# A hybrid decoder step on one core: the input projection's convolution runs one tile behind the eviction, and the delta block's last transfers are issued in the next block

## The chip, the cores and the metric

The kernel runs on one core of a Trainium2 chip. It is one program for one inference step; the metric is the device time of one execution in microseconds (us), lower is better. Five engines work on it, each through its own queue and in its order: TensorE (PE) for matmuls, with its weight loads (PEld) recorded apart; VectorE (DVE) and ScalarE (ACT) for elementwise work; GpSimd (POOL); SyncE (SP), which only issues transfers here. They wait for each other by semaphores.

## The reference, cut to what matters

The step computes two decoder layers for 512 prompt tokens and 8 sample tokens (520 columns in all) with a model width of 1024. The change touches the first layer's token mixer, a gated DeltaNet:

```python
proj = hn @ w_in                                   # hn = rms_norm(h); w_in is (1024, 4112)
qkv, z, a, b = jnp.split(proj, [A_QKV, A_QKV + A_HEADS * A_DV, A_QKV + A_HEADS * A_DV + A_HEADS], axis=-1)
full = jnp.concatenate([conv_buf, qkv], axis=1)    # 3 earlier rows ahead of it
out = sum(full[:, j:j + T] * w[j] for j in range(4))   # causal convolution, 4 taps
q, k, v = jnp.split(jax.nn.silu(out), ...)         # 8 heads of 128 each
g = -jnp.exp(A_log) * jax.nn.softplus(a + dt_bias); beta = jax.nn.sigmoid(b)
o, S = gated_delta(q, k, v, g, beta, S0)           # chunked for the prompt, one step for the samples
o = rms_norm(o, o_norm) * jax.nn.silu(z)
h = h + o @ w_out
```

The new delta states of prompt and samples and the last three rows ahead of the convolution are outputs too. After it come a dense SwiGLU, the shared keys and values, windowed attention, and an expert SwiGLU.

## The kernel before, in words

All activations lie transposed: features on the 128 partitions, 520 token columns along the free axis. Float32 products are made from three products of rounded parts: each weight and each activation is split into a high part (`w_hi`, `x_hi`, a rounding copy on ScalarE) and a low part (`w_lo`, `x_lo`, raw minus high, on VectorE), and `three_products` (L225) issues high x high, high x low, low x high, each as two matmuls of 260 columns. With 8 k-tiles an output tile of 128 features takes 48 matmuls.

Weights are streamed in chunks of 2048 elements a partition (`Stream`, L234; two output tiles for all 8 k-tiles, 1 MB, two transfers of 512 KB). There are two buffers each for raw, high and low. `load_chunk` (L202) waits on `lo_done`, so a raw buffer is filled again when the low half of the chunk two before is made. `split_hi` (L261, its instruction L265) and `split_lo` (L267, L270) make the parts.

The program is a row of blocks; a block ends on all engines before the next begins. Those around the change:

- `load_phase` (L382): inputs are loaded and turned, the first chunk is split. It clears `ab_raw`, the padded weights of the gates a and b (128 columns wide, 16 of them used), and issues their load.
- `project_in_phase` (L504): 16 chunks, 32 output tiles: 24 for q, k, v, 8 for z. PE runs `square_tensor` (L290), with the gates' product (`narrow_product`, L649) ahead of tile 1, and the wait for its eviction ahead of tile 3. The PSUM slot of a tile is t % 4. VectorE evicts a tile times the rms factor into `u` (L596), and convolves it: last tap (L615), three taps (L617), a copy of 11 edge columns (L619), the 8 sample columns' state term (L620). ScalarE puts the SiLU of `y` into `qkv` (L546) or, for z, of `u` into `z` (L577). `u` and `y` have two buffers. The order in a turn of the loop, for two chunks j: ScalarE waits for PE to be done with chunk j - 1, splits the high half of chunk j + 1, and then runs the SiLU of the chunk's two tiles; VectorE makes the low half of chunk j + 1 and then evicts and convolves the two tiles. The first four tiles are written out; the rest is a hardware loop, to tile 23 on ScalarE and VectorE and to tile 31 on PE. POOL issues two 512 KB stores of zeros after each of the first 20 convolved tiles (`expert_out`, L522). Behind tile 23 follow the gates' small steps (L563 to L570 on ScalarE, L627 to L643 on VectorE).
- `delta_phase` (L754): the delta rule for prompt and samples. SyncE's last steps are the stores of the sample states (L855), the load of the second chunk of `a_w_out` (`sp_next`), and the two stores of the prompt state (L860).
- `add_to_residual_phase` (L1652): four chunks, eight tiles of `a_w_out`. It begins with the split of chunk 0 (2048 elements at once) and of the eight tiles of its input (`Split`, L1629; instructions L1638 on ScalarE, L1649 on VectorE). SyncE loads the other chunks and, in `before_dense`, the dense stage's first.
- `dense_phase` (L1728) and what follows is not touched.

## Time and profile before

| | us |
|---|---|
| median of 3 runs | 1709.34 |
| lowest and highest | 1706.22 to 1710.46 |
| the profiled execution | 1708.81 |
| its span, first to last instruction | 1707.0 |
| PE busy in it | 1524.8 (89%) |
| VectorE, ScalarE busy | 951.7 (56%), 630.1 (37%) |
| mean granted TensorE clock | 0.926 of full speed |

The profile comes from one profiled execution. Its time is 1.8 us above its span, the part ahead of the first and behind the last recorded instruction. The busy shares are means over stages with different limits, and a PE that is shown busy may run at half its clock, so the stages have to be read one by one.

### The profile page before, as it was taken

To read this page: it belongs to the slowest core of one execution; us is meant where nothing else is said; L and a number is where in the kernel's file an instruction comes from. 1 tells how busy PE (TensorE), PEld (TensorE's weight loads), DVE (VectorE), ACT (ScalarE), POOL (GpSimd) and SP (SyncE) were. 2 spreads that over 40 slices of the span, in tenths; PEclk is the share of its full clock that TensorE was granted. 3 is DMA by queue.
4 is the path that set the end of the run, shared out by engine and by line. 5 is a ranking of instruction groups with operands and counts; after the bars stand their busy time and mean duration, and the time that the engine had idled before them with its cause. 6 is when DMAs were issued, how large, how long until landed. Compare 5 with 4: busy or idle time off the path is not lost. (4 is left out here: it accounts for less than half of the span.)

```text
span 1707.0 us, 32531 instructions
## 1 busy us (share of the span) xinstructions
PE 1524.8 (89%) x13432; PEld 1357.4 (80%) x13432; DVE 951.7 (56%) x1285; ACT 630.1 (37%) x1055; POOL 177.5 (10%) x199
## 2 busy tenths in 40 slices
PE   6988798899979999999999986467978999999994
PEld 6988797898879999999999954356876777777773
DVE  5666635666455444444345235591345677777766
ACT  4222234442143222222333110471343556566561
POOL 0111004653102000000110000000000100000002
PEclk8999998999889999999999976696878999999997
DMA  6466213000342333332333200200424888888886
GB/s 189 182 227 225 105 43 94 2 2 3 100 136 75 99 98 88 84 91 75 95 115 102 97 1 22 84 1 1 130 84 145 274 298 284 288 286 279 274 295 230
DMA packets 165509, 226.36 MB, mean 133 GB/s; under 512 B 11145, under 2 KB 130466, under 8 KB 165194
## 3 DMA queue, kind: packets, MB, share of 16 engines
q1 hardware_dynamic: 156022, 191.81, 35.1%
q0 software_dynamic: 8512, 30.48, 4.8%
q10 hardware_dynamic: 862, 2.50, 0.4%
q8 instruction: 80, 1.31, 0.3%
q14 instruction: 33, 0.26, 0.0%
HBM read 189.15 MB, written 37.88 MB: 133 GB/s over the span
## 5 line engine op out<-in xcount | busy, mean ns | idle before, releaser
L270 DVE TENSOR_TENSOR w_lo<-w_raw,w_hi 128x2048 fp32r<-128x2048 f32 x68 | 155.9, 2293 | 127.6 <-ACT w_hi L265 127.5
L265 ACT ACTIVATE w_hi<-w_raw 128x2048 fp32r<-128x2048 f32 x68 | 129.6, 1906 | 143.0 <-PE P L229 134.3
L229 PE MATMUL P<-xf_hi,w_hi 128*128 128x260 f32 x704 | 141.8, 282 | 2.0 <-DVEq L1815 1.2
L229 PE MATMUL P<-xf_hi,w_lo 128*128 128x260 f32 x704 | 141.9, 283 | 0.0
L229 PE MATMUL P<-xf_lo,w_hi 128*128 128x260 f32 x704 | 141.7, 283 | 0.0
L229 PE MATMUL P<-xa_hi,w_hi 128*128 128x260 f32 x512 | 107.9, 293 | 23.2 <-DVE w_lo L270 20.4
L229 PEld LDWEIGHTS P<-xf_hi,w_hi 128*128 128x128 f32 x704 | 108.5, 188 | 2.6 <-issue 1.4
L229 PEld LDWEIGHTS P<-xf_hi,w_lo 128*128 128x128 f32 x704 | 108.6, 188 | 0.0
L229 PEld LDWEIGHTS P<-xf_lo,w_hi 128*128 128x128 f32 x704 | 108.2, 188 | 0.0
L229 PE MATMUL P<-xa_hi,w_lo 128*128 128x260 f32 x512 | 106.3, 290 | 0.0
L229 PE MATMUL P<-xa_lo,w_hi 128*128 128x260 f32 x512 | 105.9, 289 | 0.0
L229 PEld LDWEIGHTS P<-xa_hi,w_hi 128*128 128x128 f32 x512 | 82.6, 197 | 25.3 <-issue 25.3
L2146 PE MATMUL P<-w_hi,xb_hi 128*128 128x512 f32 x344 | 102.6, 401 | 0.0
L1899 DVE TENSOR_TENSOR w_lo<-raw_more_moe,w_hi 128x1024 fp32r<-128x1024 f32 x64 | 77.1, 1223 | 41.9 <-ACT w_hi L1893 41.3
L1899 DVE TENSOR_TENSOR w_lo<-w_raw,w_hi 128x1024 fp32r<-128x1024 f32 x64 | 77.0, 1223 | 25.7 <-ACT w_hi L1893 24.8
L1893 ACT ACTIVATE w_hi<-raw_more_moe 128x1024 fp32r<-128x1024 f32 x64 | 66.1, 1054 | 45.7 <-DMA raw_more_moe<-in_moe_w_gu_dram 18.7
L229 PEld LDWEIGHTS P<-xa_lo,w_hi 128*128 128x128 f32 x512 | 82.1, 196 | 0.0
L229 PEld LDWEIGHTS P<-xa_hi,w_lo 128*128 128x128 f32 x512 | 82.0, 196 | 0.0
L1893 ACT ACTIVATE w_hi<-w_raw 128x1024 fp32r<-128x1024 f32 x64 | 67.1, 1059 | 33.2 <-DMA w_raw<-in_moe_w_gu_dram 17.0
L2025 POOL DMA_INDIRECT xb_lo<-token_rows,index x16 | 18.9, 1179 | 568.0 <-DVE index L2423 403.1
L2146 PEld LDWEIGHTS P<-w_hi,xb_hi 128*128 128x128 f32 x344 | 62.0, 188 | 19.1 <-issue 6.2
L229 PE MATMUL P<-f_hi,w_hi 128*128 128x260 f32 x352 | 70.9, 283 | 0.0
(546 smaller groups left out, 3426.8 us busy)
## 6 DMA issues: line engine op xcount, KB each, us to landing
raw_more_moe<-in_moe_w_gu_dram SPq DMA_DIRECT2D x64, 512.0 KB, 5.2
w_raw<-in_moe_w_gu_dram SPq DMA_DIRECT2D x64, 512.0 KB, 5.4
w_raw<-in_dense_w_gu_dram SPq DMA_DIRECT2D x44, 512.0 KB, 4.7
expert_out<-zeros POOLq DMA_DIRECT2D x40, 512.0 KB, 3.8
w_raw<-in_a_w_in_dram SPq DMA_DIRECT2D x32, 512.0 KB, 5.0
raw_more_moe<-in_moe_w_down_dram SPq DMA_DIRECT2D x32, 512.0 KB, 5.6
w_raw<-in_moe_w_down_dram SPq DMA_DIRECT2D x32, 512.0 KB, 5.0
w_raw<-in_dense_w_down_dram SPq DMA_DIRECT2D x16, 384.0 KB, 4.1
```

The costliest lines, as they stand in the source:

```text
L229: ins = nc.tensor.matmul(out[:, b], w, x[:, b * HALF:(b + 1) * HALF], start=(first and n == 0), stop=(last and n == 2))
L265: nc.scalar.activation(c.w_hi[:, j % 2], c.w_raw[:, j % 2], ACT.Copy).then_inc(c.hi_done, 1)
L270: nc.vector.tensor_tensor(c.w_lo[:, j % 2], c.w_raw[:, j % 2], c.w_hi[:, j % 2].bitcast(F32), ALU.subtract).then_inc(c.lo_done, 1)
L1893: nc.scalar.activation(self.hi[m % 6], self.raw[s], ACT.Copy).then_inc(self.hi_done, 1)
L1899: nc.vector.tensor_tensor(self.lo[m % 6], self.raw[m % len(self.raw)], self.hi[m % 6].bitcast(F32), ALU.subtract).then_inc(self.lo_done, 1)
L2025: pool.indirect_dma_start(out=to, out_offset=None, in_=xs[:, :], in_offset=bass.IndirectOffsetOnAxis(ap=at, axis=0)).then_inc(x_loaded[e % ...
L2146: ins = pe.matmul(c.P[:, bank + b], a[:, t], x[:, b * 512:(b + 1) * 512], start=(t == 0 and x is w_hi and a is hi), stop=(t == KT - 1 and ...
```

## The change

In the input projection:

- PE's loop is written out for all 32 tiles; the gates' product goes from ahead of tile 1 to ahead of tile 2. `square_tensor` is gone.
- ScalarE, after each eviction, copies the edge and starts `y` with the last tap (a copy scaled by a factor per partition; both were VectorE's). At odd tiles it then makes the high half of the chunk two behind the tile's own, and then, as at even tiles, the SiLU of the tile before.
- VectorE evicts tile t, then convolves tile t - 1 (state columns, three taps), and at odd tiles makes the low half. The five state operations go behind the first two splits. The gates' first steps go to tile 1, the others behind tile 27.
- `u` and `y` have three buffers instead of two; the gates' padded weights are 64 columns wide instead of 128.

At the end of the delta block SyncE's last four issues (two weight transfers of chunk 1, two stores of the prompt state) move into the next block, ahead of `st.rest`. In that block the first chunk and its low half are split in two halves of 1024 elements, and PE waits for the second one at k-tile 4.

```diff
         def _(pe):
-            def gates():
-                pe.wait_ge(ab_lo_ready, 1)
-                narrow_product(nc, pe, slot(c, 3), L.ab_hi, L.ab_lo, c).then_inc(ab_ready, 1)
-
-            def gates_taken():
-                pe.wait_ge(ab_taken, 1)
-            square_tensor(nc, c, pe, st, ready, evacuated, inward, {1: gates, 3: gates_taken})
+            for t in range(2 * st.n):
+                l = t // 2
+                if t % 2 == 0:
+                    pe.wait_ge(c.lo_done, st.number(0, l) + 1)
+                if t == 2:
+                    pe.wait_ge(ab_lo_ready, 1)
+                    narrow_product(nc, pe, slot(c, 3)[0:64], L.ab_hi, L.ab_lo, c).then_inc(ab_ready, 1)
+                if t == 3:
+                    pe.wait_ge(ab_taken, 1)
+                pe.wait_ge(evacuated, t + 1)
+                for k in range(KT):
+                    if t == 0:
+                        inward.wait_tile(c, pe, k)
+                    at = k * 256 + t % 2 * 128
...
-            def silu(m, y):
-                nc.scalar.activation(L.qkv[:, m], L.y[:, y], ACT.Silu).then_inc(y_free, 1)
-
...
-                for j in range(2):
-                    if not first or j:
-                        act.wait_ge(ready, i * 4 + 2 * j)
-                    st.split_hi(nc, c, act, i, j + 1)
-                    if first and j == 0:
-                        act.wait_ge(L.ab_loaded, 32)
-                        nc.scalar.activation(L.ab_hi[:], L.ab_raw[:], ACT.Copy).then_inc(ab_hi_ready, 1)
-                    for m in range(2):
-                        g = 2 * j + m
-                        act.wait_ge(convolved, i * 4 + (g + 1))
-                        silu(i * 4 + g, g % 2)
-            from_first(act, NQKV // 4, qkv)
-
-            act.wait_ge(ab_taken, 1)
+            def split(l):
+                if l < st.n:
+                    if l > 1:
+                        act.wait_ge(ready, 2 * l - 2)
+                    st.split_hi(nc, c, act, 0, l)
+
+            def start_convolution(t):
+                act.wait_ge(evacuated, t + 5)
+                if t >= 3:
+                    act.wait_ge(silu_done, t - 2)
+                u = L.u[:, t % 3]
+                nc.scalar.activation(L.edge[:, t], u[:, TP:TP + 11], ACT.Copy)
+                nc.scalar.activation(L.y[:, t % 3], u[:, 3:3 + NT], ACT.Copy,
+                                     scale=L.conv_w[:, 3 * NQKV + t:3 * NQKV + t + 1]).then_inc(y_started, 1)
+
+            def silu(t):
+                act.wait_ge(convolved, t + 1)
+                nc.scalar.activation(L.qkv[:, t], L.y[:, t % 3], ACT.Silu).then_inc(silu_done, 1)
+
+            split(1)
+            act.wait_ge(L.ab_loaded, 32)
+            nc.scalar.activation(L.ab_hi[:], L.ab_raw[:], ACT.Copy).then_inc(ab_hi_ready, 1)
+            for t in range(NQKV):
+                start_convolution(t)
+                if t % 2:
+                    split((t + 3) // 2)
+                if t:
+                    silu(t - 1)
             nc.scalar.activation(gb[32:40, :], ab[32:40], ACT.Sigmoid).then_inc(act_step, 1)
             nc.scalar.activation(L.a_rate[:], L.a_log[:], ACT.Exp).then_inc(act_step, 1)
-            act.wait_ge(ready, NQKV)
-            st.split_hi(nc, c, act, 0, NQKV // 2 + 1)
             act.wait_ge(dve_step, 3)
             nc.scalar.activation(t2, t2, ACT.Exp).then_inc(own_a, 1)
             act.wait_ge(own_a, 1)
             nc.scalar.activation(t2, t2, ACT.Ln, bias=1.0).then_inc(act_step, 1)
-            for l in range(NQKV // 2, st.n):
-                if NQKV // 2 < l < last:
-                    act.wait_ge(ready, 2 * l)
-                    st.split_hi(nc, c, act, 0, l + 1)
-                for t in (2 * l, 2 * l + 1):
-                    act.wait_ge(evacuated, t + 5)
-                    nc.scalar.activation(L.z[:, t - NQKV], L.u[:, t % 2, 3:3 + NT], ACT.Silu).then_inc(z_done, 1)
+            silu(NQKV - 1)
+            for t in range(NQKV, 2 * st.n):
+                act.wait_ge(evacuated, t + 5)
+                if t % 2:
+                    split((t + 3) // 2)
+                nc.scalar.activation(L.z[:, t - NQKV], L.u[:, t % 3, 3:3 + NT], ACT.Silu).then_inc(z_done, 1)
 
         @block.vector
         def _(dve):
@@ -583,6 +573,33 @@
             for k in range(KT):
...
+            def take(t):
+                dve.wait_ge(ready, t + 1)
+                if t >= 3:
+                    dve.wait_ge(convolved, min(t - 2, NQKV))
+                if t >= NQKV + 3:
+                    dve.wait_ge(z_done, t - NQKV - 2)
+                nc.vector.tensor_tensor(halves(L.u[:, t % 3, 3:3 + NT]), slot(c, t % 4), halves(rstd), ALU.mult).then_inc(evacuated, 1)
+
+            def convolve(t):
+                u, y = L.u[:, t % 3], L.y[:, t % 3]
+                dve.wait_ge(evacuated, t + 5)
+                dve.wait_ge(y_started, t + 1)
+                nc.vector.tensor_tensor(y[:, TP:NT], y[:, TP:NT], L.from_state[:, t], ALU.add)
+                for tap in (2, 1, 0):
+                    ins = nc.vector.scalar_tensor_tensor(y[:, 0:TP], u[:, tap:tap + TP],
+                                                         L.conv_w[:, tap * NQKV + t:tap * NQKV + t + 1], y[:, 0:TP], ALU.mult, ALU.add)
+                    if tap:
+                        chain.link(ins)
+                ins.then_inc(convolved, 1)
+
+            split(1)
+            dve.wait_ge(ab_hi_ready, 1)
+            nc.vector.tensor_tensor(L.ab_lo[:], L.ab_raw[:], L.ab_hi[:].bitcast(F32), ALU.subtract).then_inc(ab_lo_ready, 1)
             sw = lambda j: L.conv_w[:, j * NQKV:(j + 1) * NQKV].unsqueeze(2).broadcast_to([128, NQKV, TS])
             rows = L.conv_state[:].rearrange("p m (b j) -> p m b j", j=3)
             chain = Chain(dve, own)
...
-            def take(t, g):
-                nc.vector.tensor_tensor(halves(L.u[:, g % 2, 3:3 + NT]), slot(c, g), halves(rstd), ALU.mult).then_inc(evacuated, 1)
-
...
-                    if first and j == 0:
-                        dve.wait_ge(ab_hi_ready, 1)
-                        nc.vector.tensor_tensor(L.ab_lo[:], L.ab_raw[:], L.ab_hi[:].bitcast(F32), ALU.subtract)\
-                            .then_inc(ab_lo_ready, 1)
-                    for m in range(2):
-                        g = 2 * j + m
-                        u, y = L.u[:, g % 2], L.y[:, g % 2]
-                        tile = lambda t: t[:, ds(i * 4 + g, 1)].rearrange("p a t -> p (a t)")
-                        w = lambda tap: L.conv_w[:, ds(i * 4 + (tap * NQKV + g), 1)]
-                        dve.wait_ge(ready, i * 4 + (g + 1))
-                        take(i * 4 + g, g)
-                        dve.wait_ge(evacuated, i * 4 + (g + 5))
-                        dve.wait_ge(y_free, i * 4 + (g + 1))
-                        chain.link(nc.vector.tensor_scalar(y, u[:, 3:3 + NT], w(3), None, ALU.mult))
-                        for tap in (2, 1, 0):
-                            chain.link(nc.vector.scalar_tensor_tensor(
-                                y[:, 0:TP], u[:, tap:tap + TP], w(tap), y[:, 0:TP], ALU.mult, ALU.add))
-                        chain.link(nc.vector.tensor_copy(tile(L.edge), u[:, TP:TP + 11]))
-                        nc.vector.tensor_tensor(y[:, TP:NT], y[:, TP:NT], tile(L.from_state), ALU.add).then_inc(convolved, 1)
-                        if first and g == 0:
-                            dve.wait_ge(ab_ready, 1)
-                            nc.vector.tensor_tensor(halves(ab), slot(c, 3)[0:40], halves(rstd[0:40]), ALU.mult).then_inc(ab_taken, 1)
-            from_first(dve, NQKV // 4, qkv)
...
+            for t in range(NQKV + 1):
+                take(t)
+                if t:
+                    convolve(t - 1)
+                if t % 2:
+                    split((t + 3) // 2)
+                if t == 1:
+                    dve.wait_ge(ab_ready, 1)
+                    nc.vector.tensor_tensor(halves(ab), slot(c, 3)[0:40], halves(rstd[0:40]), ALU.mult).then_inc(ab_taken, 1)
+                    dve.wait_ge(ab_taken, 1)
+                    step.link(nc.vector.tensor_scalar(t1, t1, L.dt_bias[:], None, ALU.add))
+                    step.link(nc.vector.tensor_scalar(t2, t1, -1.0, None, ALU.mult))
+                    step.link(nc.vector.tensor_tensor(t2, t2, t1, ALU.min))
+            for t in range(NQKV + 1, 2 * st.n):
+                take(t)
+                if t % 2:
+                    split((t + 3) // 2)
+                if t == NQKV + 3:
...
@@ -847,17 +837,13 @@
             sp.wait_ge(edge_stored, 48)
             sp.wait_ge(s_scaled, 6)
             sp.wait_ge(s_masked, 2)
-            sp_next(sp, 0)
+            sp_next(sp)
             for q in (1, 3, 5, 7):
                 k, gp, _ = outers[q]
                 sp.wait_ge(s_updated, 2 * (q + 1))
                 for h in (4 * k + 2 * gp, 4 * k + 2 * gp + 1):
                     sp.dma_start(io["new_delta_sample"][0, :, h].rearrange("b k v -> k b v"), S[:, h * TS:(h + 1) * TS])\
                         .then_inc(s_stored, 16)
-            sp_next(sp, 1)
-            for g in both:
-                chain[g].after(sp, NCH - 1, dve="S")
-                sp.dma_start(io["new_delta_prompt"][0, 0, heads(g)].rearrange("h k v -> k h v"), big("S", g, NCH)).then_inc(stored, 16)
 
         @block.gpsimd
         def _(pool):
...
         def _(pe):
-            square_tensor(nc, c, pe, st, ready, evacuated, split)
+            for t in range(2 * st.n):
+                l = t // 2
+                if t % 2 == 0 and l:
+                    pe.wait_ge(c.lo_done, st.number(0, l) + 1)
+                pe.wait_ge(evacuated, t + 1)
+                for k in range(KT):
+                    if t == 0:
+                        if k == 0:
+                            pe.wait_ge(lo_half, 1)
+                        if k == KT // 2:
+                            pe.wait_ge(c.lo_done, st.number(0, 0) + 1)
+                        split.wait_tile(c, pe, k)
+                    at = k * 256 + t % 2 * 128
+                    ins = three_products(nc, slot(c, t % 4), c.w_hi[:, l % 2, at:at + 128], c.w_lo[:, l % 2, at:at + 128],
+                                         c.x_hi[:, k], c.x_lo[:, k], k == 0, k == KT - 1)
+                ins.then_inc(ready, 1)
 
         @block.scalar
         def _(act):
-            st.split_hi(nc, c, act, 0, 0)
-            split.scalar(nc, c, act)
+            act.wait_ge(c.raw_loaded[0], 32 * (st.base // 2 + 1))
+            nc.scalar.activation(c.w_hi[parts[0]], c.w_raw[parts[0]], ACT.Copy).then_inc(hi_half, 1)
+            split.high(nc, c, act, range(0, 1))
+            nc.scalar.activation(c.w_hi[parts[1]], c.w_raw[parts[1]], ACT.Copy).then_inc(c.hi_done, 1)
+            split.high(nc, c, act, range(1, KT))
             for l in range(st.n):
                 if l:
                     act.wait_ge(ready, 2 * l)
@@ -1682,8 +1685,12 @@
         @block.vector
         def _(dve):
             dve.sem_inc(evacuated, 4)
-            st.split_lo(nc, c, dve, 0, 0)
-            split.vector(nc, c, dve)
+            dve.wait_ge(hi_half, 1)
+            nc.vector.tensor_tensor(c.w_lo[parts[0]], c.w_raw[parts[0]], c.w_hi[parts[0]].bitcast(F32), ALU.subtract).then_inc(lo_half, 1)
+            split.low(nc, c, dve, range(0, 2))
+            dve.wait_ge(c.hi_done, st.base + 1)
+            nc.vector.tensor_tensor(c.w_lo[parts[1]], c.w_raw[parts[1]], c.w_hi[parts[1]].bitcast(F32), ALU.subtract).then_inc(c.lo_done, 1)
+            split.low(nc, c, dve, range(2, KT))
             for l in range(st.n):
                 if l + 1 < st.n:
...
-            ab_at = gate_at - 3 * KT * 128 * 4
-            L.ab_raw, L.ab_hi, L.ab_lo = (placed(nc, name, [128, KT, 128], dt, ab_at + i * KT * 128 * 4)
+            ab_at = gate_at - 3 * KT * 64 * 4
+            L.ab_raw, L.ab_hi, L.ab_lo = (placed(nc, name, [128, KT, 64], dt, ab_at + i * KT * 64 * 4)
...
-                    L.u, L.y, L.from_state = alloc(inner, u=[128, 2, 3 + NT], y=[128, 2, NT], from_state=[128, NQKV, TS])
+                    L.u, L.y, L.from_state = alloc(inner, u=[128, 3, 3 + NT], y=[128, 3, NT], from_state=[128, NQKV, TS])
                     project_in_phase(nc, c, Handover(c, "in", VA, (c.x_hi, c.x_lo), None, range(KT)), s_in, L, ys)
...
-                delta_phase(nc, c, io, L, lambda sp, j: s_out.load_first(c, sp, j))
+                delta_phase(nc, c, io, L, lambda sp: s_out.load_first(c, sp, 0))
             old = nc.allocated_since(before)
...
+            def at_first(sp):
+                s_out.load_first(c, sp, 1)
+                for g in range(2):
+                    sp.dma_start(io["new_delta_prompt"][0, 0, HL * g:HL * g + HL].rearrange("h k v -> k h v"),
+                                 L.delta[g]["S"][NCH % 2]).then_inc(L.stored, 16)
+
             def before_dense(sp):
                 s_gu.start(c, sp)
                 sp.wait_ge(L.s_stored, 16 * AH)
                 sp.wait_ge(L.stored, 32)
-            add_to_residual_phase(nc, c, "a_out", s_out, before_dense, Split(c, L.qkv[:, 2 * AH:3 * AH]), to_dense, s_gu)
+            add_to_residual_phase(nc, c, "a_out", s_out, at_first, before_dense, Split(c, L.qkv[:, 2 * AH:3 * AH]), to_dense, s_gu)
         [c.late] = alloc(whole, constants_late=[128, NCST - NEARLY])
         L.router, L.r_bias = alloc(whole, router=[128, KT, NE], r_bias=[128, NE])
```

## Rows read from the trace of the kernel before

**Rows 1.** Of the page: chain by engine, granted clock by slices, issues with us to landing.
```profile
PE 27%; DVE 1%; DMA 1%; issue 0%; ACT 0%; POOL 0%; SPq 0%; ACTq 0%; DVEq 0%; POOLq 0%
...
PEclk8999998999889999999999976696878999999997
...
w_raw<-in_a_w_in_dram SPq DMA_DIRECT2D x32, 512.0 KB, 5.0
```

**Rows 2.** Windows: stretch, PE, PEld, DVE, ACT, POOL busy (instructions), clock, DMA share, GB/s.
```profile
23.40:249.52 226.12, 202.96 (x1584) 200.54 (x1584) 139.62 (x212) 59.65 (x62) 21.77 (x40) 0.95 0.43 158
...
46.60:68.30 21.70, 21.70 (x183) 21.70 (x183) 15.92 (x24) 5.52 (x5) 3.17 (x6) 1.00 0.52 194
...
82.17:96.21 14.04, 11.77 (x96) 11.57 (x96) 9.72 (x17) 3.08 (x3) 2.16 (x4) 1.00 0.61 224
...
237.98:249.52 11.54, 11.50 (x96) 11.29 (x94) 1.40 (x3) 1.28 (x2) 0.00 (x0) 1.00 0.00 0
...
482.50:487.20 4.70, 4.66 (x21) 4.69 (x22) 4.70 (x8) 2.97 (x4) 0.00 (x0) 0.50 0.72 223
...
600.00:650.00 50.00, 50.00 (x418) 50.00 (x418) 20.25 (x21) 12.35 (x12) 0.00 (x0) 1.00 0.37 104
...
1400.00:1450.00 50.00, 50.00 (x395) 35.60 (x395) 37.17 (x35) 31.51 (x32) 1.82 (x2) 1.00 0.88 293
```

**Rows 3.** Waits of PE in the projection: us in total, times, longest.
```profile
PE P L229 <- DVE w_lo L270: 20.4, 10, 5.7
```

**Rows 4.** Timeline of one turn, VectorE and ScalarE: start, us, engine, line.
```profile
82.17 0.69 DVE L596 TENSOR_TENSOR u<-P,scratch 128x520 f32<-128x520 f32 x1
...
83.00 0.49 DVE L615 TENSOR_SCALAR y<-u,conv_w 128x520 f32<-128x520 f32 x1
...
83.64 2.54 DVE L617 SCALAR_TENSOR_TENSOR y<-u,conv_w,y 128x512 f32<-128x512 f32 x3
...
91.52 0.64 ACT L546 ACTIVATE qkv<-y 128x520 f32 x1 [3.95 <-DVE y L620]
...
92.07 1.90 ACT L265 ACTIVATE w_hi<-w_raw 128x2048 fp32r<-128x2048 f32 x1
...
94.00 2.29 DVE L270 TENSOR_TENSOR w_lo<-w_raw,w_hi 128x2048 fp32r<-128x2048 f32 x1 [2.60 <-ACT w_hi L265]
96.21 0.69 DVE L596 TENSOR_TENSOR u<-P,scratch 128x520 f32<-128x520 f32 x1
```

**Rows 5.** Timeline of the projection's start and its last eviction.
```profile
28.51 1.05 ACT L555 ACTIVATE ab_hi<-ab_raw 128x1024 fp32r<-128x1024 f32 x1
...
30.36 0.40 PE L229 MATMUL P<-xa_hi,w_lo 128*128 128x260 f32 x2
...
32.21 1.22 DVE L604 TENSOR_TENSOR ab_lo<-ab_raw,ab_hi 128x1024 fp32r<-128x1024 f32 x1
...
249.52 0.70 DVE L596 TENSOR_TENSOR u<-P,scratch 128x520 f32<-128x520 f32 x1 [5.07 <-PE P L229]
```

**Rows 6.** Timeline of ScalarE's gate steps.
```profile
204.51 1.28 ACT L563 ACT_TABLE_LOAD   x1
...
207.75 0.20 ACT L564 ACTIVATE a_rate<-a_log 8x1 f32<-8x1 f32 x1
```

**Rows 7.** Timeline of the delta block's end and the next block's start.
```profile
472.96 2.73 SPq L216 DMA_DIRECT2D w_raw<-in_a_w_out_dram  x2
...
474.70 0.75 DVE L1492 SCALAR_TENSOR_TENSOR qkv<-P,vec,z 128x512 f32<-128x512 f32 x1 [0.50 <-PE P L974]
475.73 1.40 SPq L860 DMA_DIRECT2D out_dram<-delta_front  x2
477.55 1.91 ACT L265 ACTIVATE w_hi<-w_raw 128x2048 fp32r<-128x2048 f32 x1 [6.62 <-PEq L837]
...
481.70 4.96 DVE L1649 TENSOR_TENSOR xo_lo<-qkv,xo_hi 128x520 fp32r<-128x520 f32 x8
...
482.54 0.77 PE L229 MATMUL P<-xo_hi,w_hi 128*128 128x260 f32 x2 [7.88 <-DVE xo_lo L1649]
...
499.42 0.71 ACT L331 ACTIVATE xf_hi<-h,vec 128x520 fp32r<-128x520 f32 x1
```

More of the change, by code:

```diff
@@ L287, in from_first @@
             body(i, False)
-def square_tensor(nc, c, pe, st, ready, evacuated, norm=None, before={}):
-    def body(i, first):
-        for j in range(2):
-            pe.wait_ge(c.lo_done, st.number(i, j) + 1)
-            for m in range(2):
-                g = 2 * j + m
-                if first and g in before:
-                    before[g]()
-                pe.wait_ge(evacuated, i * 4 + (g + 1))
-                for k in range(KT):
-                    if norm and first and g == 0:
-                        norm.wait_tile(c, pe, k)
-                    at = k * 256 + m * 128
-                    ins = three_products(nc, slot(c, g), c.w_hi[:, j, at:at + 128], c.w_lo[:, j, at:at + 128],
-                                         c.x_hi[:, k], c.x_lo[:, k], k == 0, k == KT - 1)
-                ins.then_inc(ready, 1)
-    if norm:
-        norm.tensor(c, pe)
-    from_first(pe, st.n // 2, body)
 class Handover:
@@ L506, in project_in_phase @@
     sem = lambda s: c.sem(f"in_{s}")
-    ready, evacuated, convolved, y_free, z_done, own = (sem(s) for s in ("ready", "evacuated", "convolved", "y_free", "z_done", "own"))
+    ready, evacuated, y_started, convolved, silu_done, z_done, own = (sem(s) for s in
+        ("ready", "evacuated", "y_started", "convolved", "silu_done", "z_done", "own"))
     zeros, cleared = sem("zeros"), sem("cleared")
@@ L513, in project_in_phase @@
     t1, t2, t3 = c.pair[0:AH, 0], c.pair[0:AH, 1], c.scratch[0:AH, 0]
-    last = st.n - 1
     with nc.Block() as block:
@@ L1657, in _ @@
         def _(sp):
+            sp_first(sp)
             st.rest(c, sp)
```

46 lines of the change are left out of this document (13 added, 33 removed).

## The prediction, before the changed kernel was run

> **What bounds the kernel now.** The page's chain of waits is nearly all PE, but it adds up to 29% of the span [rows 1], the end of it, and never reaches the two places that the change touches. I therefore read busy time by stretches. The input projection's matmuls run from 23.40 to 249.52 us, 226.1 us of which PE is busy 203.0, at a mean clock of 0.95; the dense stage behind it is busy 50.00 of 50.00 us [rows 2]. Time saved ahead of the dense stage is therefore not absorbed there: each block starts when the one before has ended, and PE works through it without a gap.
>
> PE's waits in the projection name one cause, the low half of the weights, 20.4 us in ten waits [rows 3]. Why it is late is seen in one turn of the loop, two tiles, in the timeline [rows 4]. VectorE evicts a tile and convolves it, twice (82.17 to 91.4, 9.2 us). Only then ScalarE runs the SiLU and the next chunk's high half (to 94.0, 2.6 us), and VectorE the low half (to 96.21, 2.2 us), and only behind that comes the next eviction. That chain is the 14.04 us of a turn. PE needs less: the last two tiles, with nothing late, take 11.54 us [rows 2], 5.77 each. In the early tiles, with the convolution running beside it, PE was busy 21.70 of 21.70 us at clock 1.00 [rows 2], so 5.77 holds under that load too.
>
> **Part one, the projection.** The change takes the chain apart: ScalarE splits the next chunk ahead of the SiLU, a tile is convolved behind the next tile's eviction, u and y get a third buffer, and the last tap and the edge copy go to ScalarE. Is anything then slower than PE's 11.54 us for two tiles?
>
> VectorE, from start to start [rows 4]: eviction 0.83, three taps 2.7, the eight state columns about 0.3, twice, and one low half 2.2: 9.9 us. ScalarE: SiLU 0.64 [rows 4]; the last tap as a copy with a factor per partition, 0.71 by the row of that form [rows 7]; the edge copy of 11 columns, which has no row on ScalarE, lies between the 0.20 of one column [rows 6] and the SiLU's 0.64 for 520, and I take 0.20, since 11 is near 1. Twice that, and 1.90 for the high half: 5.0 us, or 5.9 at the upper end. Neither binds.
>
> Then the delay from an odd tile's end R to the low half of its chunk: eviction 0.8, edge copy and tap 0.9, high half 1.9, two handovers 0.1 each put ScalarE at R + 3.8; VectorE comes free at R + 3.9 and is done at R + 6.3. PE wants that chunk two tiles on, at R + 11.5: a cover of 5.2 us. VectorE starts the next eviction some 0.4 late; four PSUM slots hide it. Were the cover gone, each us beyond it would cost 1 us a chunk.
>
> A rule speaks against moving a multiplication: the Trainium skill, ScalarE: Activation LUTs, section Rules for kernel authors, says to use VectorE for a mul, not ScalarE. The rows agree on the size for this one, 0.49 us on VectorE [rows 4] against 0.71 on ScalarE [rows 7]. Were the tap on the limiting chain, that would be 24 x 0.22 = 5.3 us and the forecast 1677; by the rows it lies under ScalarE's 6 free us a pair, and costs nothing.
>
> The start. Tile 0 is as before; its last pair ends at 30.76 [rows 5]. Tile 1 uses the same chunk and now follows at once, then the gates' product (48 matmuls of the same 260 columns, so 5.77), then tiles 2 to 31: 32 units. VectorE meanwhile does the first low half (from 28.6 to 30.9), the gates' low half (half of 1.22) [rows 5], the five state operations, moved behind these (some 2.1, the time they take now), and evicts tile 0 at about 34.3. That is 3.4 late, and tile 2's chunk is ready 11 us before its use at 42.3. The gates' eviction and three small steps end near 45; tile 3, which waits for them, starts at 48.
>
> The end. ScalarE's gate steps, four table loads of 1.28 and one- to 0.64-us operations [rows 6], with tile 23's SiLU make 7.9 us. In the new order they follow the SiLU of tile 22, from R23 + 4.5 to 12.4; z of tile 24 and the split of chunk 14 follow, and its low half is done at R23 + 17.3. PE wants it at R23 + 23.1.
>
> So the projection's last eviction comes at 30.8 + 32 x 5.77 = 215.5 us instead of 249.52 [rows 5]: **34.0 us**. Cross-check from the stretch [rows 2]: 226.1 - 203.0 = 23.1 us idle, and the missing 0.05 of clock over 226 us is 11.3, of which tile 0 keeps 1.4 (7.2 us instead of 5.8). 23.1 + 9.9 = 33.0.
>
> Loads. A turn of 14.04 us moves two halves of a chunk and four zero stores at a DMA share of 0.61; in 11.54 us that is 0.74, where the expert stage runs at 0.88 with PE full [rows 2]. A chunk is issued when the low half two chunks before is done and is wanted about 18.5 us later; landing takes 5.0 [rows 1]. Hidden, with 13 us to spare.
>
> **Part two, the end of the delta block** [rows 7]. VectorE's last result is there at 475.45. SyncE is last: behind the sample stores it issues two weight transfers (2.73) and two state stores (1.40), to 477.13, and ScalarE starts the next block at 477.55. All four now go behind the block's end, which becomes VectorE's: 475.45 + 0.35 = 475.8, 1.75 us earlier. What stands behind them in SyncE's queue: the second chunk, issued 475.9 to 478.6. If it landed as late as 7 us after, at 485.6, its halves (1.9, 2.3) would be there at 490; PE, starting near 479, wants it after two tiles, 11.5 + 2.3 for the cold start, at 492.8. And the third chunk, free to go at the first one's low half (481); the state stores have been issued by 480.1. Both hidden, the first by 2.8 us.
>
> The halved first split. Before, PE starts 482.54 - 477.55 = 5.0 us after ScalarE. After: high half of 1024 elements 1.05, low 1.22 [rows 5], x_lo 0.65, handovers 0.2: 3.1 us. That is 1.9 us. The second half is wanted at the fifth k-tile, 5.2 us after PE's start (1.3 each at the low clock), and is there after 2. Together **3.6 us**.
>
> **Sum.** 34.0 + 3.6 = 37.6. Span 1707.0 - 37.6 = 1669.4, plus the 1.8 us outside the span: 1671.2. The median of the runs shown is 0.5 above the profiled one: **1671.5 us**, 2.2% less.
>
> Two things no row prices. PE will have rested 4.3 us instead of 7.9 at the delta block's end; if it kept its clock, half of the 4.7 us at 0.50 [rows 2] would be saved, 2.3; I take nothing. And the clock of the delta stage, 8 and 9 tenths in the page's slices [rows 1], may fall otherwise when it starts 34 us earlier: I allow 4 us either way.
>
> **Rivals.**
> *Transfers bind.* If the share of 0.61 were all this mix can do, the 20 tiles with zero stores would keep 7.02 us each; 20 x 1.25 = 25 us lost, 1696. Against it: 0.72 on weights of the same row length, and 0.88 [rows 2]. 5%.
> *The order does less than it says.* A wait between ScalarE and VectorE stays in each pair, which takes 12.5 us: 12 pairs x 1 us, 1683. It needs 2.6 us more on VectorE than its rows add up to, or all 5.2 of cover gone. 6%.
> *Code loading, the slower side.* The loops become straight code: 32 units x 96 PE instructions, 12 blocks of 256. If PE stood still for a 5 us transfer at each, it would pay 60 us: 1731. It decides from 3.6 us a block. Against it: the expert stage, written out too, passes 790 PE instructions in 50 us, the same rate, with PE at 50.00 and DMA at 0.88 [rows 2]. 2%. The Trainium skill, Runtime: NRT & Kernel Launch, section Instruction fetch mechanics, has code fetched in such blocks ahead of use, with a stall only at a taken branch to code that is not there; by that rule the price is nothing, and this row agrees.
> *Something else than SyncE holds the block's end:* 1.75 lost, 1673. 5%.
>
> **How the numbers follow.** Forecast 82%, rivals as given. The low end 1664 is the clock kept (2.3) and a lucky delta stage (4), rounded out; the high end 1684 takes in an unlucky one and the second rival. About 13% lies outside. Less than 0.3% (5 us) can't be told from no change. Faster 0.96: all but the code rival and what I have not thought of; same 0.01; slower 0.03.
>
> **What would show it.** Right: evictions 5.77 us apart from tile 2 on, the last near 215.5; no wait of PE for w_lo; clock 1.00 from 31 to 215; DMA share near 0.74 while zeros are stored; the first a_out matmul 3.1 us after its block starts, and two weight issues inside that block. Wrong: a PE gap every second tile (order), gaps at every 256 PE instructions (code), w_hi waiting for a transfer (loads), a wait near tile 28 (gate steps).

## The result, and the profile after

The changed kernel takes 1671.47 us (median of 4 runs, 1670.21 to 1672.21), the kernel before beside it 1709.11 (4 runs, 1706.22 to 1710.46): ratio 0.9781, 95% interval 0.9764 to 0.9798. The forecast was 1671.5. The profiled execution of the changed kernel has a span of 1670.2 us, 36.8 less than the 1707.0 of before.

The page of the changed kernel: busy time, granted clock in 40 slices, the queue that carries code (packets, MB, share).

```profile
PE 1512.9 (91%) x13432; PEld 1347.4 (81%) x13432; DVE 932.6 (56%) x1238; ACT 648.2 (39%) x1104; POOL 177.1 (11%) x199
...
PEclk8999989998899999999999965895969999999997
...
q8 instruction: 89, 1.46, 0.4%
```

Windows of the changed kernel: the projection from tile 1 on, its part with zero stores, its part without, and the next block's first 5 us. Columns as in [rows 2].

```profile
30.60:215.50 184.90, 184.90 (x1542) 184.90 (x1541) 115.90 (x156) 72.43 (x103) 21.32 (x40) 1.00 0.55 188
42.30:157.00 114.70, 114.70 (x957) 114.70 (x956) 80.75 (x109) 44.55 (x68) 20.27 (x38) 1.00 0.74 259
157.00:215.50 58.50, 58.50 (x489) 58.50 (x489) 26.91 (x35) 24.13 (x30) 1.05 (x2) 1.00 0.21 69
444.50:449.50 5.00, 4.99 (x23) 5.00 (x24) 4.97 (x8) 4.97 (x7) 0.00 (x0) 0.50 1.01 305
```

PE is busy 184.90 of 184.90 us at clock 1.00, where before it lost 23.1 us in 226.1 and had 0.95 [rows 2]. Its waits between 22 and 262 us hold one row on the projection's line, ahead of the first matmul, and none for w_lo [rows 3]:

```profile
PE P L229 <- DVE xa_lo L313: 2.7, 1, 2.7
```

The kernel before has one more wait there that the prediction's reading left out:

```profile
PE P L229 <- DVE ab_lo L604: 2.7, 1, 2.7
```

The 23.1 us that PE lost were 20.4 for the low half of the weights and 2.7 for the low half of the gates' weights, which the changed kernel takes away by running the gates' product one tile later.

Timeline of the changed kernel: an odd tile and the even one behind it, VectorE's rows and then ScalarE's, and the last eviction. It answers to [rows 4] and [rows 5].

```profile
67.75 0.70 DVE L586 TENSOR_TENSOR u<-P,scratch 128x520 f32<-128x520 f32 x1 [2.76 <-PE P L229]
...
68.44 2.32 DVE L594 SCALAR_TENSOR_TENSOR y<-u,conv_w,y 128x512 f32<-128x512 f32 x3
71.16 2.29 DVE L270 TENSOR_TENSOR w_lo<-w_raw,w_hi 128x2048 fp32r<-128x2048 f32 x1 [0.40 <-ACT w_hi L265]
73.52 0.70 DVE L586 TENSOR_TENSOR u<-P,scratch 128x520 f32<-128x520 f32 x1
...
68.48 0.21 ACT L539 ACTIVATE edge<-u 128x11 f32<-128x11 f32 x1 [2.82 <-DVE u L586]
68.60 0.72 ACT L540 ACTIVATE y<-u,conv_w 128x520 f32<-128x520 f32 x1
69.22 1.90 ACT L265 ACTIVATE w_hi<-w_raw 128x2048 fp32r<-128x2048 f32 x1
...
217.68 0.70 DVE L586 TENSOR_TENSOR u<-P,scratch 128x520 f32<-128x520 f32 x1 [5.07 <-PE P L229]
```

The low half is done 5.7 us behind the odd tile's end (67.75 to 73.45), and the high half now starts before the convolution ends (69.22 against 70.76), where before it started behind it. The 2.76 us at 67.75 are time in which VectorE has nothing to do but wait for PE: PE sets the pace.

Timeline of the changed kernel at the end of the delta block and the next block's start, beside [rows 7]:

```profile
440.39 0.75 DVE L1478 SCALAR_TENSOR_TENSOR qkv<-P,vec,z 128x512 f32<-128x512 f32 x1 [0.52 <-PE P L960]
441.42 0.95 SPq L216 DMA_DIRECT2D w_raw<-in_a_w_out_dram  x2
441.44 1.06 ACT L1668 ACTIVATE w_hi<-w_raw 128x1024 fp32r<-128x1024 f32 x1 [4.84 <-PEq L827]
...
442.42 1.05 SPq L3047 DMA_DIRECT2D out_dram<-delta_front  x2
...
444.51 0.77 PE L229 MATMUL P<-xo_hi,w_hi 128*128 128x260 f32 x2 [4.16 <-DVE xo_lo L1632]
```

From VectorE's last result to PE's first matmul it is now 3.4 us (441.14 to 444.51); before it was 7.1 (475.45 to 482.54) [rows 7].

**Where the 36.8 us come from.** The projection, from its first matmul to its last eviction, went from 226.1 us (23.40 to 249.52) to 192.5 (25.21 to 217.68): 33.6. The first matmul stood 1.8 us later. The delta block, from that eviction to VectorE's last result, took 223.5 us instead of 225.9: 2.5. The turn between the blocks gave 3.7. From there to the end it took 1225.7 instead of 1224.5: 1.2 lost. 33.6 - 1.8 + 2.5 + 3.7 - 1.2 = 36.8. Only 33.6 and 3.7 belong to the change. The kernels below (but for experiment 10, which adds work there) had their first matmul anywhere from 22.9 to 26.0 us, and their delta block took from 223.2 to 226.0 us whatever was changed, so a span alone moves by some 3 us.

### The profile page after: what moved, and what is told of

It is laid out like the page before. It is cut to its first block and busy times, and to the rows that moved or that the text cites. A ratio compares the mean times of both kernels' runs of the same rounds, so it can differ in the third digit from the quotient of the medians.

```text
span 1670.2 us, 32194 instructions
## 1 busy us (share of the span) xinstructions
PE 1512.9 (91%) x13432; PEld 1347.4 (81%) x13432; DVE 932.6 (56%) x1238; ACT 648.2 (39%) x1104; POOL 177.1 (11%) x199
## 5 line engine op out<-in xcount | busy, mean ns | idle before, releaser
L229 PE MATMUL P<-xa_hi,w_hi 128*128 128x260 f32 x512 | 104.0, 285 | 2.7 <-DVE xa_lo L313 2.7
```

Source lines behind the costliest of these rows:

```text
L229: ins = nc.tensor.matmul(out[:, b], w, x[:, b * HALF:(b + 1) * HALF], start=(first and n == 0), stop=(last and n == 2))
```

## The experiments

All times are medians, each with its ratio to the kernel before on the same chip. The experiments ran on four chips, so between two of them the ratios compare better than the microseconds. "Changed" is the changed kernel, and a diff is against it unless another is named.

**1. The projection alone.** The kernel before, with only the projection block of the changed one (its tensor, scalar and vector parts, buffers of three, gates' weights of 64 columns); the delta block's end and the block behind it as before.

> The new input projection alone; the delta block's end and the first split behind it are as before. Both parts add up (the prediction): 34.0 us less than before, 1675, and the projection's evictions come 5.77 us apart with no wait of PE for w_lo. If the second part did nothing: 1671, as fast as the whole change. If the parts overlapped, so that one alone gave most of it: under 1673.

1675.53 us, 0.9812 (0.9794 to 0.9831). The projection took 193.1 us (25.96 to 219.10) and the turn between the blocks 7.1 again. So the projection alone gives 31.8 us by the medians and 33.0 by its own length. What is left for the turn is 4 to 6 us by the medians, which fits the 3.7 of the trace but can't show it.

**2. The old order, written out.** The kernel before's order of operations, but with its loops unrolled in the program, as the changed kernel's are. PE's two-turn loop in the block behind the delta block is written out too.

```
+def written_out(eng, n, body):
+    body(0, True)
+    for i in range(1, n):
+        body(i, False)
-    from_first(pe, st.n // 2, body)
+    written_out(pe, st.n // 2, body)
...
-            from_first(act, NQKV // 4, qkv)
+            written_out(act, NQKV // 4, qkv)
...
-            from_first(dve, NQKV // 4, qkv)
+            written_out(dve, NQKV // 4, qkv)
```

> The kernel before, with its order and its two buffers, but the projection's loops written out instead of run by the hardware loop (in the delta block's next block too, which has only two turns). In the profile of before a written-out turn (evictions at 55.45 and 68.06) takes 12.6 us and a looped one 14.04. Theory, the order is a serial chain: a turn takes 12.6, never 11.54; ten turns at 1.4 less give 14 us, 1695, and PE still waits for w_lo. Rival, the loop alone was the cause: turns of 11.54 and 1675 to 1678. Rival, the loop costs nothing: 1709.

1694.95 us, 0.9924 (0.9903 to 0.9944). With no change of order this gives 12.4 us, a third of the gain; in the profiled execution the projection itself is 15.4 shorter, and its first matmul 2.4 later. Its timeline over one turn of two tiles:

```profile
70.57 0.69 DVE L603 TENSOR_TENSOR u<-P,scratch 128x520 f32<-128x520 f32 x1
71.30 0.49 DVE L622 TENSOR_SCALAR y<-u,conv_w 128x520 f32<-128x520 f32 x1
71.82 2.33 DVE L624 SCALAR_TENSOR_TENSOR y<-u,conv_w,y 128x512 f32<-128x512 f32 x3
...
80.97 2.29 DVE L270 TENSOR_TENSOR w_lo<-w_raw,w_hi 128x2048 fp32r<-128x2048 f32 x1 [2.51 <-ACT w_hi L265]
83.18 0.69 DVE L603 TENSOR_TENSOR u<-P,scratch 128x520 f32<-128x520 f32 x1
```

A turn is 12.61 us (70.57 to 83.18), against 14.04 in the loop [rows 4]. The durations are the same; the gaps are not. By groups of one turn each, first the kernel before (82.17 to 96.21), then this one (70.57 to 83.18); the last number ahead of a releaser is idle time:

```profile
L617 DVE SCALAR_TENSOR_TENSOR y<-u,conv_w,y 128x512 f32<-128x512 f32 x6 | 4.5, 751 | 0.9
```

```profile
L624 DVE SCALAR_TENSOR_TENSOR y<-u,conv_w,y 128x512 f32<-128x512 f32 x6 | 4.5, 752 | 0.2
```

The six taps cost 0.9 us of gaps in the loop and 0.2 written out. PE still waits for the low half, 10.7 us in nine waits, so the chain of [rows 4] is still what binds, and 2.6 us once for the gates' low half. The rest of the gain comes with the new order, the later product of the gates included. Which of the engines' loops costs the gaps, and why, wasn't tried.

**3. The last tap back on VectorE** (the edge copy stays on ScalarE).

```
-                nc.scalar.activation(L.edge[:, t], u[:, TP:TP + 11], ACT.Copy)
-                nc.scalar.activation(L.y[:, t % 3], ..., scale=...).then_inc(y_started, 1)
+                nc.scalar.activation(L.edge[:, t], u[:, TP:TP + 11], ACT.Copy).then_inc(y_started, 1)
...
+                chain.link(nc.vector.tensor_scalar(y, u[:, 3:3 + NT], L.conv_w[...], None, ALU.mult))
```

> The changed kernel with the last tap back on VectorE; the edge copy stays on ScalarE. By the rows VectorE then needs 9.9 + 1.1 to 1.3 = 11.1 us for two tiles, under PE's 11.54, and the low half is ready at R + 7.0 instead of 6.3 where PE wants it at R + 11.5: no change, 1671.5. Rival, the tap's move is what the gain needs: VectorE over 11.54 a pair, each 0.5 us over it costs 6 us, 1677 or more.

**4. Two buffers for u and y** instead of three (every `% 3` is `% 2`, every wait one tile sooner).

> The changed kernel with two buffers for u and y instead of three. In the new order the convolution of tile t - 2 is done before tile t is evicted, so nothing waits for the third buffer: no change, 1671.5. Rival, the third buffer carries part of the gain: ScalarE's start of y waits for the SiLU two tiles before and VectorE with it, 12 pairs by 1 us or more, 1683.

The third gave 1669.66 us, 0.9782 (0.9761 to 0.9803), the fourth 1672.01, 0.9788 (0.9764 to 0.9812). Neither differs from the changed kernel. In the third the projection took 192.2 us (22.86 to 215.02), in the fourth 193.2 (25.51 to 218.70). Neither the tap on ScalarE nor the third buffer is needed for the gain, each taken back by itself; both together weren't tried.

**5 and 6. How much cover the low half has.** ScalarE makes two, or four, further copies of the whole chunk ahead of each high half, 1.95 us each.

```
...
+                        for _ in range(2):
+                            more.link(nc.scalar.activation(c.w_hi[:, l % 2], c.w_raw[:, l % 2], ACT.Copy))
                     st.split_hi(nc, c, act, 0, l)
```

> The changed kernel, with the high half of chunks 2 to 15 made three times over by ScalarE (2 x 1.9 + 0.1 us more at each odd tile, the result is the same). It measures the cover: in the trace of after the low half is done 5.8 us after the odd tile's end, wanted at 11.5. 5.8 + 3.9 = 9.7, still covered: no change, 1671.5. Rival, there is no such cover and a delay at this point goes to PE: 14 x 3.9 us, 1726, or part of it.

> The same with four more (7.8 us at each odd tile): 5.8 + 7.8 = 13.6, 2.1 beyond the cover. By the prediction's sentence each us beyond costs a us a chunk: 14 x 2.1 = 29 us, 1701. Rival: a late chunk also moves the tile that its successor counts from, so only half of the overshoot is paid, (13.6 + 11.54) / 2 = 12.6 a pair, and ScalarE's own work is 5.0 + 7.8 = 12.8 a pair: 14 x 1.1 to 1.3 = 15 to 18 us, 1687 to 1690.

Two more: 1681.63 us, 0.9857 (0.9833 to 0.9880). Four more: 1736.35, 1.0176 (1.0157 to 1.0195). Both expectations missed: two copies were to cost nothing and cost 10 us, and four missed the upper forecast of 1701 by 35 us. The projection took 204.7 us (25.01 to 229.67) and 257.2 (25.44 to 282.61), 12.2 and 64.7 more than in the changed kernel. Timeline of the kernel with two more over one pair, VectorE and then ScalarE:

```profile
63.76 2.29 DVE L270 TENSOR_TENSOR w_lo<-w_raw,w_hi 128x2048 fp32r<-128x2048 f32 x1 [4.30 <-ACT w_hi L265]
65.97 0.69 DVE L591 TENSOR_TENSOR u<-P,scratch 128x520 f32<-128x520 f32 x1
...
66.65 2.32 DVE L599 SCALAR_TENSOR_TENSOR y<-u,conv_w,y 128x512 f32<-128x512 f32 x3
68.89 0.70 DVE L591 TENSOR_TENSOR u<-P,scratch 128x520 f32<-128x520 f32 x1
...
76.19 2.29 DVE L270 TENSOR_TENSOR w_lo<-w_raw,w_hi 128x2048 fp32r<-128x2048 f32 x1 [4.30 <-ACT w_hi L265]
78.40 0.69 DVE L591 TENSOR_TENSOR u<-P,scratch 128x520 f32<-128x520 f32 x1
...
69.00 0.64 ACT L550 ACTIVATE qkv<-y 128x520 f32<-128x520 f32 x1 [1.48 <-DVE y L599]
69.61 0.21 ACT L544 ACTIVATE edge<-u 128x11 f32<-128x11 f32 x1
69.73 0.71 ACT L545 ACTIVATE y<-u,conv_w 128x520 f32<-128x520 f32 x1
70.35 3.85 ACT L536 ACTIVATE w_hi<-w_raw 128x2048 fp32r<-128x2048 f32 x2
74.24 1.92 ACT L265 ACTIVATE w_hi<-w_raw 128x2048 fp32r<-128x2048 f32 x1
```

No VectorE row but the low half waits for anything, and ScalarE waits for VectorE: the rows form a closed circle. Low half 2.2, the even tile's eviction 0.6, the convolution of the odd tile before it 2.4, that tile's SiLU 0.6, the next odd tile's edge and tap 0.7, the copies 3.9, the high half 1.95, and the low half again: 12.43 us (63.76 to 76.19), more than PE's 11.54. The odd tile's eviction ends together with that SiLU (69.59 and 69.64), so the circle closes as fast through VectorE's own order. With four copies a turn of it is 16.3 us (from one of these low halves to the next):

```profile
72.44 2.29 DVE L270 TENSOR_TENSOR w_lo<-w_raw,w_hi 128x2048 fp32r<-128x2048 f32 x1 [8.20 <-ACT w_hi L265]
...
88.75 2.29 DVE L270 TENSOR_TENSOR w_lo<-w_raw,w_hi 128x2048 fp32r<-128x2048 f32 x1 [8.18 <-ACT w_hi L265]
```

Less the copies both leave 8.5 us: that is the circle in the changed kernel, and its room is 11.54 - 8.5 = 3.0 us a pair, not 5.2. The changed kernel's own trace shows nearly that, the 2.76 us that VectorE waits for PE at each odd tile.

**7 and 8. Does the circle explain it?** One copy more, which leaves the circle below PE's pace; and two more with the circle opened, by another order on ScalarE at odd tiles (diff against the kernel with two more).

```
             for t in range(NQKV):
+                if t % 2:
+                    split((t + 3) // 2)
+                    if t > 1:
+                        silu(t - 2)
                 start_convolution(t)
                 if t % 2:
-                    split((t + 3) // 2)
-                if t:
                     silu(t - 1)
```

> The changed kernel with one further whole copy of the chunk (1.95 us) on ScalarE ahead of each high half of the input projection. Theory of the closed circle (low half 2.2, eviction and taps of VectorE 2.9, SiLU 0.6, edge and tap 0.7, high half 1.9, handovers: 8.5 us for two tiles, against PE's 11.54): 8.5 + 1.95 = 10.5 is still below 11.54, so no change against the changed kernel: 1671 to 1672 us, and no wait of PE for w_lo. Rival, each microsecond put on ScalarE here costs part of itself by other ways (half of the 10 us that two copies cost): 1676 us.

> The kernel with two further copies (3.9 us) ahead of each high half, but ScalarE's order at an odd tile changed: the copies and the high half stand ahead of the SiLU and of the odd tile's edge and tap, so that they wait for PE's last matmul on the old chunk and not for VectorE's convolution. Theory of the closed circle: the convolution and the SiLU leave it; what is left is low half 2.2, eviction 0.7, edge and tap 0.8, copies and high half 5.8, 9.6 with handovers, below 11.54: back to 1671 to 1673 us, evictions 5.77 apart, no wait of PE for w_lo. Rival, the copies themselves cost (a further 3.9 us on ScalarE a chunk, or its reads beside VectorE's and the loads'): 1681 us, as in the kernel with two further copies in the changed kernel's order.

One more: 1672.25 us, 0.9797 (0.9783 to 0.9811), no wait for w_lo, and VectorE idles 0.96 us ahead of an odd tile's eviction where the circle leaves 11.54 - 10.5 = 1.0:

```profile
66.85 0.70 DVE L591 TENSOR_TENSOR u<-P,scratch 128x520 f32<-128x520 f32 x1 [0.96 <-PE P L229]
```

The opened circle: 1675.23, 0.9810 (0.9794 to 0.9825), 6 us less than with the same copies inside it (8 by the ratios). Its timeline shows PE setting the pace:

```profile
68.10 0.70 DVE L593 TENSOR_TENSOR u<-P,scratch 128x520 f32<-128x520 f32 x1 [0.47 <-PE P L229]
...
79.63 0.70 DVE L593 TENSOR_TENSOR u<-P,scratch 128x520 f32<-128x520 f32 x1 [0.48 <-PE P L229]
...
68.10 3.87 ACT L536 ACTIVATE w_hi<-w_raw 128x2048 fp32r<-128x2048 f32 x2 [1.91 <-PE P L229]
```

The high half now waits for PE, and the pair is 11.53 us (68.10 to 79.63). It came out 2 us above the band expected. PE waits once for w_lo, 1.1 us ending at 195.99, for the chunk that ScalarE splits behind its gate steps; the projection took 193.9 us (25.49 to 219.34), 1.4 more than in the changed kernel. The delta block, which is the same in both, took 225.8 (219.34 to 445.12) instead of 223.5, which is within what the block varies by. These two are more than the 2 us.

**9. Do transfers bind?** Every zero store is made twice, the second into a buffer of its own in HBM.

```
-                pool.dma_start(ys[i * 128:(i + 1) * 128], L.zeros[:]).then_inc(cleared, 16)
+                for to in (ys, more):
+                    pool.dma_start(to[i * 128:(i + 1) * 128], L.zeros[:]).then_inc(cleared, 16)
...
```

> The changed kernel with every store of zeros done twice, the second time into a second buffer: the DMA share over the first 20 tiles would have to be 0.74 + 0.46 = 1.2, more than there is. Theory, the projection has room in its transfers because only weights are waited for and they are wanted 18 us after they are issued: the stores fall behind and end later, inside the projection (they have 58 us behind tile 20 with little else), PE does not wait, 1671.5 to 1674. Rival, transfers bind once the share is full: the 20 tiles take 1.2 x 5.77 = 6.9 us each, 23 us more, 1694.

1672.13 us, 0.9797 (0.9780 to 0.9815). The window with zero stores:

```profile
42.60:157.00 114.40, 114.40 (x955) 114.40 (x954) 79.13 (x107) 44.72 (x68) 40.16 (x76) 1.00 0.99 383
```

The DMA share went from 0.74 to 0.99 and the rate from 259 to 383 GB/s, and PE is still busy 114.40 of 114.40 us. Transfers don't bind at 0.74.

**10. Keeping PE's clock over the turn between the blocks.** PE multiplies the identity, 8 times at the projection block's start and 13 times at the next block's.

```
+            for _ in range(13):
+                pe.matmul(c.P[:, 7, 0:128], cols(c, CI), cols(c, CI), start=True, stop=True)
```

> The changed kernel, with 8 matmuls of the identity (128 columns, into a slot that is not in use) ahead of tile 0 of the projection and 13 ahead of tile 0 of the block behind the delta block, where PE waits for the first split. In the trace of after PE runs at half clock for about 3 us at the first place and 4.9 (444.5 to 449.5) at the second. Theory, the clock rises after some time of work and not of products that count: 1.7 and 3.0 us of it would be spent ahead of time, half of that is gained, about 2.3 us in sum: 1669. Rival, short f32 matmuls do not raise it: 1671.5. Rival, they hold the first real matmul back: 1673.

1672.97 us, 0.9804 (0.9786 to 0.9822): no gain. The first matmuls on the weights:

```profile
445.88 0.52 PE L229 MATMUL P<-xo_hi,w_hi 128*128 128x260 f32 x2
446.25 0.40 PE L229 MATMUL P<-xo_lo,w_hi 128*128 128x260 f32 x2
```

They run at 0.40 us a pair at once, at the upper of the two clock levels (granted 0.99 over the block's first 5 us), where the changed kernel's take 0.64 for some 5 us at the lower one (0.50). But the 13 products were recorded as 26, and ran from 440.34 to 446.2. The block started 1.1 us sooner than in the changed kernel, so PE could have begun at 443.4 and began at 445.9. The block's eight tiles took 2.2 us less from there, so 2.2 us of clock were won and 2.5 of start lost. At the projection's start it came out about even too: the 8 products were recorded as 16, PE began 1.5 us later behind ScalarE's start than in the changed kernel, and the projection was 1.9 us shorter (190.5). Smaller numbers weren't tried.

**11. The first split whole; 12. the four transfers back in the delta block.** Five rounds each.

```
-            nc.scalar.activation(c.w_hi[parts[0]], c.w_raw[parts[0]], ACT.Copy).then_inc(hi_half, 1)
-            split.high(nc, c, act, range(0, 1))
-            nc.scalar.activation(c.w_hi[parts[1]], c.w_raw[parts[1]], ACT.Copy).then_inc(c.hi_done, 1)
-            split.high(nc, c, act, range(1, KT))
+            st.split_hi(nc, c, act, 0, 0)
+            split.high(nc, c, act, range(0, KT))
...
```

> The changed kernel with the first split behind the delta block whole again (2048 elements, then the eight tiles), while the four transfers stay moved. Theory: PE's first matmul comes 5.0 us after the block's start instead of 3.1, 1.9 us more: 1673.4. Rival, the second half is what PE waits for anyway: 1671.5.

```
-            sp_next(sp)
+            sp_next(sp, 0)
...
+            sp_next(sp, 1)
+            for g in both:
+                chain[g].after(sp, NCH - 1, dve="S")
+                sp.dma_start(io["new_delta_prompt"][...], big("S", g, NCH)).then_inc(stored, 16)
...
```

> The changed kernel with the four transfers issued in the delta block again; the split stays halved. Theory, SyncE holds the block's end: from VectorE's last result to ScalarE's first instruction 2.1 us instead of 0.3 to 0.4, 1.75 us more, 1673.2. Rival, SyncE's two weight issues (0.95 us in the trace of after, not 2.73) were slow only by chance and the block ends with VectorE: 1671.5 to 1672.

1671.04 us, 0.9798 (0.9785 to 0.9811), and 1672.13, 0.9792 (0.9778 to 0.9805). The medians can't tell either from the changed kernel (0.9781, 0.9764 to 0.9798): an effect of 1.8 us is below what they resolve. At PE's first matmul the traces can. With the split whole, ScalarE starts at 440.99 and PE at 445.98: 4.99 us, against 3.07 (441.44 to 444.51), 1.9 more. With the transfers back, the timeline has

```profile
438.58 2.73 SPq L216 DMA_DIRECT2D w_raw<-in_a_w_out_dram  x2
441.36 1.40 SPq L850 DMA_DIRECT2D out_dram<-delta_front  x2
...
443.19 1.06 ACT L1672 ACTIVATE w_hi<-w_raw 128x1024 fp32r<-128x1024 f32 x1 [6.63 <-PEq L827]
```

and VectorE's last result at 441.10, so ScalarE starts 2.1 us behind it, against 0.3: 1.8 more. Both sizes are those of the prediction.

They don't last to the block's end. In these two traces PE's clock rose sooner behind its first matmul (0.70 and 0.68 over 5 us, against 0.50 in the changed kernel), and the block's last eviction comes only 1.0 us later, counted from the delta block's end, than in the changed kernel, in each. Whether the later start has to do with that is open: the clock over the projection's first 5 us was anything from 0.50 to 0.63 in kernels with the same code there. From the kernel before to the changed one, with both changes, the block's last eviction did gain 3.6 us.

## Why the prediction was right, and where it was not

**The time.** The terms held: 34.0 us for the projection measured 33.6, 3.6 for the turn 3.7. That the median meets the forecast to 0.1 us is luck all the same. The prediction's own sum ends at 1671.2 + 0.5 = 1671.7, not 1671.5, and the stretches that the change doesn't touch moved by -1.8, 2.5 and -1.2 us and nearly cancel.

**The bound.** Right. Time saved ahead of the dense stage was not absorbed: the 36.8 us are accounted for above, and the stages behind the change differ by 1.2 us.

**The pace of 5.77 us a tile.** Right: 192.5 us for the projection where the steps gave 34.0 of 226.1 less, 192.1. Clock 1.00 and the DMA share of 0.74 came out as worked out. The last eviction was put at 215.5 and came at 217.68; 1.8 of the 2.2 us is the later first matmul.

**ScalarE's edge copy and tap.** Priced at 0.20 and 0.71, measured 0.21 and 0.72. The Trainium skill's rule (ScalarE: Activation LUTs, section Rules for kernel authors) would take the tap back to VectorE; experiment 3 did, and the time stayed the same, as the free time of both engines had it.

**VectorE's sum.** 9.9 us of work a pair was worked out; the changed kernel has 8.4 (11.53 less the 2.76 and 0.40 us that VectorE waits). The terms were taken from start to start in the loop, and so had its gaps in them.

**The gate steps.** The low half behind them was put at R + 17.3 of tile 23 and came at R + 16.4 (171.55 to 187.97), ahead of PE's use of it; PE doesn't wait there.

**The gain was put on the order alone.** This is a gap in the explanation, not in the sum. PE's waits were said to name one cause; they name two, and 2.7 us were for the gates' low half. The sum went by PE's pace and so held whatever removed the wait. But the turn of 14.04 us was read as a chain of work, and 1.4 us of it is gaps that go once the loop is written out. Experiment 2 gives the shares by the projection's own length: 226.1 us before, 210.7 written out (25.81 to 236.50), 192.5 with the order as well. That is 15.4 for writing out and 18.2 for all the rest of the change in the projection: the order, and in it the wait of 2.6 us for the gates that the later product takes away. The moved state operations, the moved gate steps and the narrower gate weights weren't tried by themselves, nor was the changed order written as a loop, so what the order would give alone stays open.

**The cover of 5.2 us.** This is the step that failed. The distance from the low half's end to PE's use of it was worked out nearly right (R + 5.7 measured, R + 6.3 worked out), but it isn't the room. VectorE works in order, and behind a late low half stand the next even tile's eviction and the convolution; the next high half waits for their results. The circle closes at 8.5 us, so only 3.0 us a pair are free, and beyond that each us costs one a pair (a turn of 12.43 us with 3.9 us of copies, 16.3 with 7.8). Two copies were expected to cost nothing and cost 10 us, four were expected to cost 15 to 30 and cost 65. The rival "the order does less" was priced from the 5.2 too, so its threshold was put too far off; the changed kernel is nearer to it than the text had it. It did not come to that in the changed kernel, so the time was right.

**Transfers, code.** Transfers don't bind (experiment 9). Code neither: in the 184.90 us without a gap PE passes 1542 matmuls and 1541 weight loads of the written-out program, where the rival wanted a stop at each 256 instructions. By the Trainium skill, Runtime: NRT & Kernel Launch, section Instruction fetch mechanics, straight code is fetched ahead; the trace agrees: the instruction queue carried 89 packets, 80 in the kernel before, and PE never stopped for one.

**The turn between the blocks.** 3.6 us predicted, 3.7 measured at PE's first matmul, 1.8 by the transfers and 1.9 by the split when each is taken back alone (experiments 11 and 12). A detail was wrong: the two weight transfers were to take SyncE 2.7 us again and took 0.95, so that the cover of the second chunk was more than the 2.8 us given. That PE starts at its lower clock was taken, and the window above has it at 0.50 for 5 us.

## What to carry to other kernels

An engine that works in order closes circles: to know how much a step may be late, add up the whole way round from the step to itself, through both engines, and compare that with the pace of the bound; the distance to the next use of its result is only an upper end. When a change both reorders work and writes a loop out, time the old order written out as well, because the gaps of the loop can be nearly half of what the order seems to give (15.4 of 33.6 us here). An effect of 2 us in 1670 is read from its own place in the trace, since medians of five rounds can't show it; and it is read again at the end of its block, since part of it may be gone by then.

## What the runs showed of the hardware

- The same vector operations have the same duration in a loop and written out (751 and 752 ns), but the gaps ahead of them differ: 0.9 us and 0.2 us for six. Over a turn of two tiles the difference was 1.4 us of 14.04. What makes the gaps wasn't isolated.
- Two issues of 512 KB took SyncE 2.73 us directly behind the sample stores (in the kernel before and in experiments 1 and 12) and 0.95 us when they came 3 us later. What shortens them wasn't isolated.
- PE stayed at 114.40 busy of 114.40 us beside a DMA share of 0.99 and 383 GB/s.
- A matmul of plain f32 on a 128x128 identity was recorded as two: 13 gave 26, in 5.8 us, begun while PE's clock was at its lower level.
- With the same code, PE's granted clock over the projection's first 5 us differed from run to run, from 0.50 to 0.63.
